# Pairs of 64-row score matmuls and pairs of 64-column value matmuls in a two-block transformer kernel

## What is computed

```python
# first block, gated delta net: queries and keys are normalised, and two gates are made
gq, gk = l2_normalize(gq), l2_normalize(gk)
beta = jax.nn.sigmoid(gdn_b)
g = -jnp.exp(a_log) * jax.nn.softplus(gdn_a + dt_bias)

# second block, branch a (8 heads of 64, 2 key heads), b (8 heads, 2 key heads), c (4 heads, 2 maps each)
sc = jnp.einsum('bqkgd,bskd->bkgqs', qblk, k); p = softmax(sc); o = einsum('bkgqs,bskd->bqkgd', p, v)   # a
sc = einsum(q, kband) + bias;  p = exp(sc - m) / (sum + exp(sink - m)); o = einsum(p, vband)            # b
p = softmax(sc + bias);  attn = p[map 0] - lam * p[map 1];  o = einsum(attn, v)                         # c
branches = einsum('bsnw,nwd->bsnd', ys, w_branch); merged = sum(sigmoid(gate_logits) * branches)
```

## Time and profile before

| | us |
|---|---|
| three runs, median | 2559.8 |
| profiled execution, device time | 2557.38 |
| its span, first to last instruction | 2555.6 |
| granted TensorE clock, share of full | 0.998 |
| TensorE busy | 2523.4 |
| VectorE busy | 1544.5 |
| ScalarE busy | 1352.7 |
| GpSimd busy | 274.4 |

### The profile page before, as it was taken

The page is one execution under the profiler, slowest core; times in us unless marked ns, Lnnn a source line. Parts: engine busy times, 40 slices in busy tenths (PEclk is TensorE's granted clock), DMA queues, the critical chain, the costliest instruction groups (busy, mean ns, idle before and its releaser), DMA issues.

```text
span 2555.6 us, 46929 instructions
## 1 busy us (share of the span) xinstructions
PE 2523.4 (99%) x18718; PEld 2374.0 (93%) x18718; DVE 1544.5 (60%) x2034; ACT 1352.7 (53%) x2077; POOL 274.4 (11%) x180
## 2 busy tenths in 40 slices
PE   9999999999999999999999999999999999999998
PEld 8989998999899899899989989999999988999997
DVE  5658646566565774656656656457655655557664
ACT  5447546554544672655545445565445445565543
POOL 0200111000000002200100000552000000345000
PEclk9999999999999999999999999999999999999999
DMA  6655314465565541348755555335665665435664
GB/s 241 202 183 172 113 67 134 140 198 196 198 197 191 173 157 58 108 140 198 222 192 188 195 173 174 116 116 182 197 194 185 193 194 174 133 108 166 194 193 140
DMA packets 118377, 428.02 MB, mean 167 GB/s; under 512 B 13164, under 2 KB 14956, under 8 KB 117804
## 3 DMA queue, kind: packets, MB, share of 16 engines
q1 hardware_dynamic: 117696, 424.82, 51.6%
q10 hardware_dynamic: 492, 0.46, 0.1%
HBM read 423.79 MB, written 1.44 MB: 166 GB/s over the span
## 4 chain that ended last, share of the span: by engine, by line
PE 91%; DVE 5%; ACT 2%; issue 1%; DMA 1%; DVEq 0%; POOL 0%; ACTq 0%; SPq 0%; POOLq 0%
PE bank L484 39%; PE bank L695 38%; DVE lo_slots L472 2%; PE bank L1005 2%; PE bank L1672 2%; PE bank L504 2%; PE bank L1711 1%; PE bank L1160 1%; PE bank L634 1%; PE bank L1688 1%; PE bank L1171 1%; ACT hi_slots L458 1%; PE bank L1169 1%; DVE conv_out L967 1%; PE bank L1854 1%
## 5 line engine op out<-in xcount | busy, mean ns | idle before, releaser
L472 DVE TENSOR_TENSOR lo_slots<-raw,hi_slots 128x1024 fp32r<-128x1024 f32 x732 | 903.4, 1240 | 688.6 <-ACT hi_slots L458 687.9
L458 ACT ACTIVATE hi_slots<-raw 128x1024 fp32r<-128x1024 f32 x788 | 830.7, 1059 | 727.1 <-PE bank L695 426.0
L695 PE MATMUL bank<-x_hi_room,hi_slots 128*128 128x256 f32 x2816 | 783.2, 278 | 2.1 <-DVE x_lo_room L664 1.6
L695 PE MATMUL bank<-x_lo_room,hi_slots 128*128 128x256 f32 x2816 | 781.3, 277 | 0.0
L695 PE MATMUL bank<-x_hi_room,lo_slots 128*128 128x256 f32 x2816 | 781.3, 277 | 0.0
L695 PEld LDWEIGHTS bank<-x_hi_room,hi_slots 128*128 128x128 f32 x2816 | 529.7, 188 | 4.2 <-issue 3.9
L695 PEld LDWEIGHTS bank<-x_lo_room,hi_slots 128*128 128x128 f32 x2816 | 531.6, 189 | 0.1
L695 PEld LDWEIGHTS bank<-x_hi_room,lo_slots 128*128 128x128 f32 x2816 | 530.3, 188 | 0.0
L484 PE MATMUL bank<-x_hi_room,hi_slots 128*128 128x256 f32 x1152 | 331.6, 288 | 2.3 <-DVE x_lo_room L664 1.8
L484 PE MATMUL bank<-x_hi_room,lo_slots 128*128 128x256 f32 x1152 | 320.6, 278 | 0.0
L484 PE MATMUL bank<-x_lo_room,hi_slots 128*128 128x256 f32 x1152 | 320.5, 278 | 0.0
(11 more groups left out here) (339 smaller groups left out, 3314.4 us busy)
## 6 DMA issues: line engine op xcount, KB each, us to landing
raw<-w_full SPq DMA_DIRECT2D x792, 512.0 KB, 4.2
bias_mem<-bias_rows SPq DMA_DIRECT2D x8, 288.0 KB, 7.9
mem<-mem_t SPq DMA_DIRECT2D x2, 1024.0 KB, 8.3
const<-consts SPq DMA_DIRECT2D x1, 1664.0 KB, 9.4
h<-x_t SPq DMA_DIRECT2D x2, 512.0 KB, 7.2
final<-finals SPq DMA_DIRECT2D x2, 512.0 KB, 7.4
out_t<-h SPq DMA_DIRECT2D x4, 256.0 KB, 2.7
bias_rows<-junk ACTq DMA_DIRECT2D x1, 384.0 KB
```

What stands on the lines that cost most here:

```text
L458: nc.scalar.activation(w_hi[s], raw[s][:, :], ACT.Copy).then_inc(hi_ready[s], 1)
L472: nc.vector.tensor_tensor(w_lo[s], raw[s][:, :], w_hi[s].bitcast(F32), ALU.subtract).then_inc(lo_ready[s], 1)
L695: mm = nc.tensor.matmul(out, lhsT=w[:, part], rhs=x[:, k, :], start=k == 0 and b % 2 == 0 and n == 0, stop=k == KT - 1 and b % 2 == 1 and ...
```

## The change

- Scores: at every even step the maps i and i + 1 are computed together, each from the 64 rows that hold its head, into the two banks, in the order token half 0 map i, token half 0 map i + 1, token half 1 map i, token half 1 map i + 1. The step waits until both maps of the pair before have left their banks. The odd steps have no scores. The zero-padded keys and their making on GpSimd are gone, the rotated keys stay in `qa[:, 4]`.
- Values of a and b: at every odd step the values of a whole pair are multiplied, each with 64 stationary columns, into the upper and the lower half of one bank's partitions. The even steps have none. Branch c stays as it was.
- Gates of the delta net: VectorE splits three units, does the two gate operations, splits the fourth and takes the two reciprocals last; TensorE waits for both reciprocals ahead of the first of the eight matmuls.

```diff
-            for i in range(2):
-                split_lo(E, E.mid(4, 2 * i))
-                split_lo(E, E.mid(4, 2 * i + 1))
-                dve.wait_ge(sems["gdn_root"], E.after("gdn_root", i + 1))
-                nc.vector.reciprocal(gdn_sq[:, 0, tile_cut(i)], ...).then_inc(sems["gdn_rec"], 1)
+            for s in range(SLOTS - 1):
+                split_lo(E, E.mid(4, s))
             dve.wait_ge(sems["ab_tp"], E.after("ab_tp", 1))
             ...
             nc.vector.tensor_scalar(pre[:, :, 4:8], ...).then_inc(sems["gate_dve"], 1)
+            split_lo(E, E.mid(4, SLOTS - 1))
+            for i in range(2):
+                dve.wait_ge(sems["gdn_root"], E.after("gdn_root", i + 1))
+                nc.vector.reciprocal(gdn_sq[:, 0, tile_cut(i)], ...).then_inc(sems["gdn_rec"], 1)
...
-                if i < len(maps):
-                    m = maps[i]
-                    if i >= 2:
-                        if maps[i - 2]["kind"] in "bc":
-                            pe.wait_ge(sems["s_bias"], E.after("s_bias", 2 * maps[i - 2]["biased"] + 2))
+                if i < len(maps) and i % 2 == 0:
+                    two = maps[i:i + 2]
+                    for n in range(i - 2 if i else 0, i):
+                        if maps[n]["kind"] in "bc":
+                            pe.wait_ge(sems["s_bias"], E.after("s_bias", 2 * maps[n]["biased"] + 2))
                         else:
-                            pe.wait_ge(sems["s_exp"], E.after("s_exp", 2 * (i - 1)))
+                            pe.wait_ge(sems["s_exp"], E.after("s_exp", 2 * (n + 1)))
                     for t in range(TT):
-                        mm = nc.tensor.matmul(bank[4 + i % 2][:, tile_cut(t)], lhsT=m["q"][:, t * P:(t + 1) * P], rhs=m["k"],
-                                              start=True, stop=True)
-                    mm.then_inc(sems["s_ps"], 1)
+                        for r, m in enumerate(two):
+                            mm = nc.tensor.matmul(bank[4 + r][:, tile_cut(t)], lhsT=m["q"][:, t * P:(t + 1) * P], rhs=m["k"],
+                                                  start=True, stop=True)
+                            if t == TT - 1:
+                                mm.then_inc(sems["s_ps"], 1)
...
-                        for kt in range(TT):
-                            mm = nc.tensor.matmul(bank[pair % 2][:, 0:TOK], lhsT=vab[:, 2 * kt + (m["kind"] == "b"), at:at + P],
-                                                  rhs=weights[kt], start=u % 2 == 0 and kt == 0,
-                                                  stop=u % 2 == 1 and kt == TT - 1)
-                    mm.then_inc(sems["y_ps"], 1)
+                        for kt in range(TT):
+                            for r in range(2):
+                                rows, at = slice(r * HEAD_DIM, (r + 1) * HEAD_DIM), 2 * r * HEAD_DIM
+                                mm = nc.tensor.matmul(bank[pair % 2][rows, 0:TOK],
+                                                      lhsT=vab[:, 2 * kt + (m["kind"] == "b"), at:at + HEAD_DIM],
+                                                      rhs=probs_t[:, r, tile_cut(kt)], start=kt == 0, stop=kt == TT - 1)
+                                if kt == TT - 1:
+                                    mm.then_inc(sems["y_ps"], 1)
...
-                for r in range(0 if a < 4 else 2):
-                    rows = slice(r * HEAD_DIM, (r + 1) * HEAD_DIM)
-                    nc.vector.tensor_tensor(rope_k[rows, r, :], rope_t[rows, 0, cols], rope_t[rows, 1, cols],
-                                            ALU.add).then_inc(sems["rope"], 1)
...
-                    if g == 4:
-                        pool_keys(E, E.mid(5, g))
```

More of the change, by code:

```diff
@@ L135 @@
     "go_sb": (4, 0), "ds_ps": (3, 0), "state_dve": (5, 0),
-    "pads": (2, 9),
+    "pads": (2, 1),
     "z_ps": (8, 0), "sp_act": (24, 0), "lb": (8, 0), "lm": (8, 0), "lm_causal": (8, 0), "btw_ps": (8, 0),
@@ L1110, in pe_gdn @@
             pe.wait_ge(sems["gate_dve"], E.after("gate_dve", 2))
+            pe.wait_ge(sems["gdn_rec"], E.after("gdn_rec", 2))
             for i in range(2):
-                pe.wait_ge(sems["gdn_rec"], E.after("gdn_rec", i + 1))
                 for hd in range(GDN_HEADS):
@@ L1611, in mix2_maps @@
             maps = []
-            for kind, q, keys in (("a", qa, rope_k), ("b", qb, kb)):
+            for kind, both in (("a", qa), ("b", qb)):
                 for i in range(HEADS):
                     b, r = divmod(i, 2)
-                    maps.append(dict(kind=kind, head=b + 4 * r, r=r, q=q[:, b, :], k=keys[:, r, :]))
+                    rows = slice(r * HEAD_DIM, (r + 1) * HEAD_DIM)
+                    maps.append(dict(kind=kind, head=b + 4 * r, r=r, q=both[rows, b, :], k=both[rows, 4, :]))
             for i in range(2 * C_HEADS):
                 hd, r = divmod(i, 2)
-                maps.append(dict(kind="c", head=HEADS + hd, q=qc[:, hd, :], k=kc[:, hd // 2 * 2 + r, :]))
+                rows = slice(r * HEAD_DIM, (r + 1) * HEAD_DIM)
+                maps.append(dict(kind="c", head=HEADS + hd, q=qc[rows, hd, :], k=qc[rows, 4 + hd // 2, :]))
             return maps
@@ L1693, in pe_attention @@
                     u = m["use"]
-                    pe.wait_ge(sems["pt_sb"], E.after("pt_sb", u + 1))
-                    weights = [probs_t[:, u % 2, tile_cut(kt)] for kt in range(TT)]
                     if m["kind"] == "c":
+                        pe.wait_ge(sems["pt_sb"], E.after("pt_sb", u + 1))
+                        weights = [probs_t[:, u % 2, tile_cut(kt)] for kt in range(TT)]
                         hd = m["head"] - HEADS
@@ L1704, in pe_attention @@
                                                   rhs=weights[kt], start=kt == 0, stop=kt == TT - 1)
-                    else:
+                        mm.then_inc(sems["y_ps"], 1)
+                    elif u % 2:
                         pair = u // 2
-                        if pair >= 2 and u % 2 == 0:
+                        pe.wait_ge(sems["pt_sb"], E.after("pt_sb", u + 1))
+                        if pair >= 2:
                             pe.wait_ge(sems["y_lo"], E.after("y_lo", pair - 1))
-                        at = m["r"] * HEAD_DIM
                         for kt in range(TT):
-                            mm = nc.tensor.matmul(bank[pair % 2][:, 0:TOK], lhsT=vab[:, 2 * kt + (m["kind"] == "b"), at:at + P],
-                                                  rhs=weights[kt], start=u % 2 == 0 and kt == 0,
-                                                  stop=u % 2 == 1 and kt == TT - 1)
-                    mm.then_inc(sems["y_ps"], 1)
+                            for r in range(2):
[4 more added lines that the diff above has]
+                                if kt == TT - 1:
+                                    mm.then_inc(sems["y_ps"], 1)
                 for g in gates_at(E, i):
@@ L2416, in _ @@
                         pe_mix2_project(E)
-                        pe.wait_ge(sems["rope"], E.after("rope", 4))
+                        pe.wait_ge(sems["rope"], E.after("rope", 3))
                         for s in range(SLOTS):
```

39 lines of the change are left out of this document (6 added, 33 removed).

## The result

| | before | after |
|---|---|---|
| median of 14 runs each, us | 2563.17 | 2546.43 |
| lowest and highest | 2557.76, 2571.86 | 2541.44, 2556.89 |
| ratio with 95% interval | | 0.9933 [0.9918, 0.9948] |
| profiled execution, device time, us | 2557.38 | 2546.65 |
| its span | 2555.6 | 2544.9 |

The kernel is faster by 17.2 us with an interval of 13.3 to 21.0 (1 - 0.9933 of 2563.17, and so for both ends). The forecast was 2545.5, a gain of 14.3.

The account below looks back on a forecast made before the run. TensorE's own sequence, busy in 99% of the span, was taken as the bound. Attention 11.0 us (a layer 5.5 + 4.0 - 3.8 - 0.15) plus gates 3.3 made 14.3: 2559.8 - 14.3 = 2545.5 us, own range 2541 to 2550, wider range 2537 to 2553.

Parts of the forecast that it names:

- Price of a pair of scores: Attention scores: eight records in four waves plus 0.40 us switch, 1.26 instead of 1.72; 12 pairs a layer save 5.5 us.
- Price of a pair of values: Values in branches a and b: 0.86 plus 0.36 us switch, 1.22 instead of 1.72; 8 pairs a layer save 4.0 us.
- The strict order: Rival: matmuls start in program order, so a pair needs five waves, 0.215 us more; total 2552.2 us, chance 0.11.
- the halves that don't overlap: Rival: 64-row halves run in turn, a pair of scores costs 0.40 us more, values 0.36; total 2576 us, chance 0.05.
- The cheap switch: Rival: going in and out of tiles costs 0.1 us, not 0.40 and 0.36; 2535.7 us, half of that 2540.6; chance 0.10.
- The wait in b: Branch b transposes: TensorE arrives at T + 4.54 us, probabilities allow T + 5.50; waits 0.96 four times a layer, 3.8.
- The wait in a: Branch a transposes: ScalarE leads, probabilities allow T + 4.53 + 0.06 us; TensorE waits 0.05 three times a layer.
- the prediction's own sign of being wrong: Waits at transposes (L1688) in a or c, first full matmul over 0.5 us after a pair's last wave, or delta net no earlier.
- Odd maps hidden: Odd steps: ScalarE's copy waits for the pair's values; probabilities done at 5.0 us, needed at 5.76, 0.7 to spare.
- The longer chain: Rival: ScalarE falls over 0.7 us behind in b's odd steps, each pair gives back 1.0; total 2553.5 us, chance 0.05.
- Gates: Delta net: gate operations ahead of the reciprocals remove group 6's (L504) waits of 1.81 and 1.5 us, 3.3 in all.
- It changes nothing: Rival: gate waits come back later and half of the pairs' gain is lost; total 2556 us, chance 0.03.

Follow-up runs that it names:

- e7: Kernel after with all score records of one map ahead of the other's; attention stage 114.96 / 114.85 us, one execution of 2557.32 us.
- e6: Kernel after with branch b's sink left out, so another result; attention stage 111.91 / 111.94 us, ratio to before 0.9905.
- e8: Kernel after with a pair's values behind the even step's gate unit and the sink's maximum by TENSOR_REDUCE; stage 109.19 / 109.42 us, ratio to before 0.9890.
- e3: Kernel before with only the new order of the delta net's gates; gates 6.89 / 6.89 us, attention 121.25 / 121.25, ratio to before 0.9973.
- e2: Kernel after with a pair's values moved behind the gate unit of the even step; attention stage 113.94 / 114.02 us, ratio to before 0.9926.

## Why the prediction was right

- *Where the time is.* TensorE's own sequence bounds the kernel, and each of the 40 pairs paid. This step held.
- *Price of a pair of scores:* forecast 1.26, measured 1.21. The switch in and out of tiles, taken at 0.40 from 32-row tiles, is 1.21 - 0.86 = 0.35 for 64 rows.
- *Price of a pair of values:* forecast 1.22, measured 1.21; switch 0.36 forecast, 0.35 measured. With both prices a pair of a should be 10.0 - 0.51 - 0.51 = 8.98 long without a wait. It is 8.79: the two gate units give 0.2 more by their shorter step, which the prediction had at nothing.
- *Four waves, not five:* shown by the starts in after, and by e7 for any order of the records. The strict order is out; so are the halves that don't overlap. The cheap switch is out with 0.35.
- *The wait in b:* forecast 0.96 four times a layer. The view has 0.94, 1.03, 1.03 and 1.07 in layer 0, 4.1 for 3.8, but the forecast reckons from start to start, and so it measured 1.10, 1.19, 1.19 and 1.23, 4.7. The chain was right: with T = 1630.13 + 0.12 the transposes start at T + 5.48 for 5.50. TensorE is there at T + 4.39 and not 4.54, by the cheaper switch and the shorter gate unit, and in three pairs GpSimd's split adds 0.1 to the chain. It is the term that decides the sum: with a chain shorter by 0.7 (e6) the stage loses 3.0 us more, with the wait gone (e8) 5.5 to 5.8. e6 shows that the chain through VectorE and ScalarE makes it.
- *The wait in a:* forecast three of 0.05. The view has one of 0.22 at the first pair; from start to start it is 0.38, and the third and fourth pair are late by 0.14 each, 0.7 for 0.15. In the first pair one of the scaling operations took 0.85 us for its usual 0.35, for a reason that is open; in the others TensorE came earlier than reckoned. By the prediction's own sign of being wrong, waits in branch a, this term failed, though it is small.
- *Odd maps hidden:* ScalarE's copy waits for the values at odd steps as told (1637.49 in step 9, behind the values of 1636.32), and the odd maps' transposes have no wait in after. The 0.7 us to spare was enough, even with a sink operation of 1.15 us for 0.23, which I had not foreseen. The longer chain is out.
- *Branch c:* no new wait, as forecast. A pair gives 0.60 us where 0.46 was forecast, with the shorter steps in it.
- *Gates:* forecast 1.8 + 1.5 = 3.3, measured 1.85 + 1.3 = 3.2, and nothing given back later (e3).
- *Sum:* the attention gave 6.3 us a layer, forecast 5.5. From start to start the waits grew by 5.4 and 5.3 us a layer where 3.95 was forecast, so TensorE's work fell by 11.7 and 11.6 for 9.5. Of these 2.1 to 2.2 more, a cheaper switch is 12 x 0.05 + 8 x 0.01 = 0.7 and the shorter step of the gate units 1.5 to 1.6. So the mechanism holds term by term, but two misses, 2.2 of saving that was not foreseen and 1.4 of waiting, stand against each other, and that the sum is only 0.8 off is in part luck. The stages together are 15.8 for 14.3, and the timed 17.2 [13.3, 21.0] holds both.
- *A slip in the rivals:* "It changes nothing" is put at 2556; without the 3.3 of the gates and half of the 11.0 it is 2559.8 - 5.5 = 2554.3.

## What to carry to other kernels

Two matmuls that use half of the array each can run as tiles side by side, float32 with its two records too; count the waves, and add what going in and out costs (0.35 us for a group of eight records here). When a step is moved so that TensorE gets faster, work out for the very next consumer when its input is ready: the gain of one part and the gain of another are paid out of the same slack, and here 5.4 us of 11.7 a layer went back that way. Read such a wait from start to start: an idle time that is counted from a matmul's modelled end is too short by what a record lasts beyond its step. Where a small VectorE operation is in a chain that decides and GpSimd works on SBUF beside it, look at its min, median and max, and not only at the mean.

## What the runs showed of the hardware that I had not expected

A VectorE TENSOR_SCALAR on 128 x 2 numbers in SBUF, started while GpSimd had a split of 2.4 us in work, ended only with it: 1.16 to 1.18 us for 0.23, in 14 of 16 cases in e2. In after operations with two SBUF inputs were slower too when they started beside GpSimd (0.68 us became 1.65 to 1.76 in the delta net, 0.69 became 2.49 in a rotation), and not when they started ahead of it (0.69 at 298.00, GpSimd from 298.16). It did not hold for TENSOR_REDUCE (0.69 as ever) nor for an addition with one input in PSUM (0.42). The Trainium skill ("SBUF — State Buffer", "Who interferes with whom") says that VectorE and GpSimd share one pair of ports as a lock held for the whole instruction, that a `tensor_scalar` in a two-port mode takes it, that an operation with two SBUF inputs contends with a GpSimd instruction that reads SBUF, and that on trn2 a reduction never contends. The traces agree with what it says of the two kinds of inputs and of the reduction; which mode the `tensor_scalar` ran in no trace shows. e8 against e2 puts the price of the lock here at 4.6 to 4.8 us a layer, of which at most 8 x 0.07 = 0.6 is that the reduction itself is shorter.

TensorE reorders: of two halves of the array it serves the free one, whatever the order in the program (e7). The first wave of a tiled group takes 0.32 us to the second with scores and 0.27 with values, where the later ones are 0.215 apart. And full-array matmuls keep one of two steps, 0.113 or 0.118 us, for a whole unit of 24 at a time in the attention; over an execution the mix of the two made 11 us of difference between kernels with the same matmuls (after and e7).
